# A hybrid decoder layer on one core: the first norm on two token tiles at a time, with another first chunk of projection weights

## The reference, cut to what matters

```python
def reference(x, mix_norm, w_in, ...):              # x: 1 x 512 x 1024, float32
    h = rms_norm(x, mix_norm)                       # the first norm: one root per token
    z = h @ w_in                                    # columns aq ak av iq ik iw pin gu gv sq sk sv gl
    o_a = sparse_indexed_attention(aq, ak, av, iq, ik, iw, ...)   # indexer scores, top 128 keys, attention
    o_b = multiscale_pool(pin, ...)
    o_c = chunked_spatial_gating(gelu(gu), gelu(gv), ...)
    o_d = stick_breaking_attention(sq, sk, sv)
    x = x + (sum of sigmoid(gl_n) * (o_n @ w_branch[n])) @ w_out
    return x + swiglu_ffn(rms_norm(x, ffn_norm), w_ffn_gate, w_ffn_up, w_ffn_down)

# the indexer of branch A, for each block of 128 queries:
head_scores = relu(einsum('bthd,bsd->bths', q_idx, k_idx))        # 8 heads
idx_score = einsum('bth,bths->bts', w_idx, head_scores)
```

## Time and profile before

| | |
|---|---|
| median of 3 runs | 811.78 us |
| the profiled execution | 811.23 us, of which the span from first to last instruction is 809.3 us |
| TensorE (PE) busy | 789.0 us, 97% of the span |
| VectorE (DVE) busy | 502.2 us, 62% |
| ScalarE (ACT) busy | 375.8 us, 46% |
| GpSimd (POOL) busy | 59.3 us, 7% |
| matmuls | 4713 |
| DMA | 80.36 MB, mean 99 GB/s |

### The profile page before, as it was taken

The page is one execution under the profiler, slowest core; times in us unless marked ns, Lnnn a source line. Parts: engine busy times, 40 slices in busy tenths (PEclk is TensorE's granted clock), DMA queues, the critical chain, the costliest instruction groups (busy, mean ns, idle before and its releaser), DMA issues.

```text
span 809.3 us, 11519 instructions
## 1 busy us (share of the span) xinstructions
PE 789.0 (97%) x4713; PEld 692.5 (86%) x4713; DVE 502.2 (62%) x743; ACT 375.8 (46%) x525; POOL 59.3 (7%) x71
## 2 busy tenths in 40 slices
PE   3999999999999999999989999999999999999998
PEld 3899887877778878878878889999988899999886
DVE  5535987656577566361284699888633478887331
ACT  5435544577845533522233465555521245554210
POOL 6000040000000050050060000000000000000000
PEclk9999999999999999999999999999999999999999
DMA  8452213121122313513314213333232233333321
GB/s 256 123 164 67 92 53 104 53 96 62 53 59 97 104 53 104 208 54 104 104 53 150 85 53 122 111 110 111 101 125 91 74 97 104 106 104 104 120 89 52
DMA packets 63763, 80.36 MB, mean 99 GB/s; under 512 B 1684, under 2 KB 51936, under 8 KB 63712
## 3 DMA queue, kind: packets, MB, share of 16 engines
q1 hardware_dynamic: 63376, 79.18, 30.6%
q0 software_dynamic: 336, 0.46, 0.2%
HBM read 75.96 MB, written 2.10 MB: 96 GB/s over the span
## 4 chain that ended last, share of the span: by engine, by line
PE 78%; issue 13%; POOL 3%; DVE 3%; ACT 1%; DMA 1%; SPq 0%; POOLq 0%; DVEq 0%
PE bank L1378 16%; PE bank L1380 16%; PE bank L1379 16%; PE bank L1745 8%; PE bank L1747 8%; PE bank L1746 8%; POOL merged L483 3%; PE bank L1544 1%; PE bank L1553 1%; DMA x_sb<-in_x_dram 1%; DVE w_lo L863 1%; PE bank L1484 1%; PE bank L1458 0%; PE bank L1528 0%; ACT h_hi L527 0%
## 5 line engine op out<-in xcount | busy, mean ns | idle before, releaser
L863 DVE TENSOR_TENSOR w_lo<-raw,w_hi 128x2048 fp32r<-128x2048 f32 (+1 forms) x45 | 100.2, 2228 | 121.1 <-ACT w_hi L503 120.8
L1378 PE MATMUL bank<-h_hi,w_hi 128*128 128x512 f32 (+1 forms) x392 | 150.7, 385 | 0.7 <-DVE h_lo L1186 0.5
L1380 PE MATMUL bank<-h_hi,w_lo 128*128 128x512 f32 (+1 forms) x392 | 149.3, 381 | 0.0
L1379 PE MATMUL bank<-h_lo,w_hi 128*128 128x512 f32 (+1 forms) x392 | 149.1, 380 | 0.0
L503 ACT ACTIVATE w_hi<-raw 128x2048 fp32r<-128x2048 f32 (+1 forms) x49 | 91.1, 1861 | 89.0 <-PE bank L1380 88.1
L1745 PE MATMUL bank<-t_hi,w_hi 128*128 128x256 f32 x320 | 89.7, 280 | 0.0
L1746 PE MATMUL bank<-t_lo,w_hi 128*128 128x256 f32 x320 | 89.3, 279 | 0.0
L1747 PE MATMUL bank<-t_hi,w_lo 128*128 128x256 f32 x320 | 89.3, 279 | 0.0
L1378 PEld LDWEIGHTS bank<-h_hi,w_hi 128*128 128x128 f32 x392 | 73.7, 188 | 15.4 <-issue 1.3
L1380 PEld LDWEIGHTS bank<-h_hi,w_lo 128*128 128x128 f32 x392 | 73.7, 188 | 14.3
L1379 PEld LDWEIGHTS bank<-h_lo,w_hi 128*128 128x128 f32 x392 | 73.7, 188 | 13.6
(11 more groups left out here) (232 smaller groups left out, 1473.5 us busy)
## 6 DMA issues: line engine op xcount, KB each, us to landing
raw<-in_w_in_dram SPq DMA_DIRECT2D x26, 1024.0 KB, 5.2
raw<-in_w_ffn_gate_dram SPq DMA_DIRECT2D x11, 1024.0 KB, 5.3
raw<-in_w_ffn_up_dram SPq DMA_DIRECT2D x11, 1024.0 KB, 5.3
raw<-in_w_ffn_down_dram SPq DMA_DIRECT2D x10, 1024.0 KB, 5.0
raw<-in_w_branch_dram SPq DMA_DIRECT2D x4, 1024.0 KB, 4.8
raw<-in_w_out_dram SPq DMA_DIRECT2D x4, 1024.0 KB, 5.1
x_sb<-in_x_dram SPq DMA_DIRECT2D x4, 512.0 KB, 5.0
x_sb<-in_x_dram SPq DMA_DIRECT2D x1, 2048.0 KB, 10.5
```

Source lines behind the costliest of these rows:

```text
L863: vec.tensor_tensor(w_lo[:, at], raw[:, c % 2, 0:n], w_hi[:, at].bitcast(F32), ALU.subtract)\
L1378: mm(dst, l_hi, r_hi, start=start, stop=False)
L1379: mm(dst, l_hi, r_lo, start=False, stop=False)
L1380: return mm(dst, l_lo, r_hi, start=False, stop=stop)
```

## The change

`aq` becomes chunk 0, of a new kind "first"; `ik` and `iq` become chunks 1 and 2, and from `ak` (3) on the numbers stay. The first norm is made on token tiles 0 and 1, then on tiles 2 and 3, and each half is followed by its half of the matmuls of `aq`. `aq` is loaded in two halves, right behind tiles 0 and 1 of x; the seven loads of `vrow` go to GpSimd's queue. IDX_SLOT becomes 3, so that the indexer's blocks stand in slots 3, 4, 5, the early splits are those of chunks 5 to 8, and in chunk 6 (rows, two parts) both pairs of heads stand between the parts. The turns of slot 1 go to slot 2. `gv` and `gu` get another place in SBUF. Waits that count squares are moved by one, since there is one more square on ScalarE.

```diff
+    chunks.append(("first", in_cols(w_in, col["aq"]), KT, CW, "aq"))
     chunks.append(("rows", in_cols(w_in, col["ik"], P), KT, P, "ik"))
     chunks.append(("rows", in_cols(w_in, col["iq"]), KT, CW, "iq"))
-    for n in ("aq", "ak", "av", "gv"):
+    for n in ("ak", "av", "gv"):
...
-        gv = place("gv", [P, TT, MIX], at=X0)
-        gu = place("gu", [P, MT, SEQ], at=X0 + 4 * KB)
...
+        gv = place("gv", [P, TT, MIX], at=L0 + 44 * KB)
+        gu = place("gu", [P, MT, SEQ], at=L0 + 48 * KB)
         act_junk = place("act_junk", [P, 2, D], at=L0)
-        dve_junk = place("dve_junk", [P, 2, D], at=L0 + 20 * KB)
+        dve_junk = place("dve_junk", [P, 1, D], at=L0 + 20 * KB)
...
-        IDX_SLOT = 2
+        IDX_SLOT = 3
...
-            for t in range(TT):
+            def load_x(t):
                 sp.dma_start(x_sb[:, t, :], x[0, t * P:(t + 1) * P, :]).then_inc(x_ready[t], 16)
+            def load_first(half, ready):
+                src = chunks[0][1][:, half * KT // 2:(half + 1) * KT // 2, :]
+                dst = raw[:, 0, half * CHUNK // 2:(half + 1) * CHUNK // 2].rearrange("p (k c) -> p k c", c=CW)
+                sp.dma_start(dst, src).then_inc(ready, 16)
 
             def load(c):
                 _, src, nk, cols, _ = chunks[c]
@@ -367,18 +374,17 @@
                 dst = raw[:, c % 2, 0:nk * cols].rearrange("p (k c) -> p k c", c=cols)
                 sp.dma_start(dst, src).then_inc(raw_ready[c % 2], 16)
 
-            load(0)
-            sp.dma_start(vrow[0:KT, :], mix_norm[0].rearrange("(k p) -> k p", p=P)).then_inc(S["vec_in"], 16)
-            sp.dma_start(vrow[PSC:PSC + MT, :], pool_scale[0].rearrange("(k p) -> k p", p=P)).then_inc(S["vec_in"], 16)
-            sp.dma_start(vrow[GMN:GMN + MT, :], gmlp_norm[0].rearrange("(k p) -> k p", p=P)).then_inc(S["vec_in"], 16)
-            for r, g in ((QN, attn_q_norm), (KN, attn_k_norm)):
-                for j in range(2):
-                    sp.dma_start(vrow[r:r + 1, j * HEAD_DIM:(j + 1) * HEAD_DIM], g).then_inc(S["vec_in"], 16)
+            load_x(0)
+            load_x(1)
+            load_first(0, S["w_first"])
+            load_first(1, raw_ready[0])
+            load_x(2)
+            load_x(3)
             for c in range(1, MIXER_CHUNKS):
                 load(c)
                 if c == 4:
 
-                    wait_chunk_taken(sp, 1)
+                    wait_chunk_taken(sp, 2)
...
+            pool.dma_start(vrow[0:KT, :], mix_norm[0].rearrange("(k p) -> k p", p=P)).then_inc(S["vec_in"], 16)
+            pool.dma_start(vrow[PSC:PSC + MT, :], pool_scale[0].rearrange("(k p) -> k p", p=P)).then_inc(S["vec_in"], 16)
+            pool.dma_start(vrow[GMN:GMN + MT, :], gmlp_norm[0].rearrange("(k p) -> k p", p=P)).then_inc(S["vec_in"], 16)
+            for r, g in ((QN, attn_q_norm), (KN, attn_k_norm)):
+                for j in range(2):
+                    pool.dma_start(vrow[r:r + 1, j * HEAD_DIM:(j + 1) * HEAD_DIM], g).then_inc(S["vec_in"], 16)
...
-            for t in (0, 2):
+            def squares_of(t):
                 act.wait_ge(x_ready[t], 16)
-                nact.activation(act_junk[:, t // 2, :], x_sb[:, t, :], ACT.Square, accum_out=stat[:, t:t + 1])\
+                nact.activation(act_junk[:, t % 2, :], x_sb[:, t, :], ACT.Square, accum_out=stat[:, t:t + 1])\
                     .then_inc(S["squares_summed"], 1)
-            take_root(slice(0, TT))
-            split(0)
-            act.wait_ge(S["rstd_ready"], 1)
-            nact.activation(x_sb[:, TT - 1, :], x_sb[:, TT - 1, :], ACT.Copy, scale=rstd[:, TT - 1:TT])\
-                .then_inc(S["h_last_scaled"], 1)
+            def scaled(t):
+                act.wait_ge(S["rstd_ready"], t // 2 + 1)
+                nact.activation(x_sb[:, t, :], x_sb[:, t, :], ACT.Copy, scale=rstd[:, t:t + 1])\
+                    .then_inc(S["h_last_scaled"], 1)
+            def first_high(half, arrived):
+                at = slice(half * CHUNK // 2, (half + 1) * CHUNK // 2)
+                act.wait_ge(arrived, 16)
+                nact.activation(w_hi[:, at], raw[:, 0, at], ACT.Copy).then_inc(hi_ready if half else S["first_hi"], 1)
+            def h_high(half, ks):
+                cols = slice(half * SEQ // 2, (half + 1) * SEQ // 2)
+                for k in ks:
+                    n = half * KT + k
+                    act.wait_ge(S["h_turned"], n + 1)
+                    nact.activation(h_hi[:, k, cols], bank[4 + n % 4][:, 0:SEQ // 2], ACT.Copy,
+                                    scale=vcol[:, MIXN + k:MIXN + k + 1]).then_inc(S["h_hi_ready"], 1)
+            squares_of(0)
+            take_root(slice(0, 2))
+            first_high(0, S["w_first"])
+            scaled(1)
             act.wait_ge(S["vec_turned"], 1)
-            link(nact.activation(vcol[:, :], bank[1][:, 0:VECS], ACT.Copy))
-            for k in range(KT):
-                act.wait_ge(S["h_turned"], k + 1)
-                nact.activation(h_hi[:, k, :], bank[2 + k % 6][:, :], ACT.Copy, scale=vcol[:, MIXN + k:MIXN + k + 1])\
-                    .then_inc(S["h_hi_ready"], 1)
+            link(nact.activation(vcol[:, :], bank[3][:, 0:VECS], ACT.Copy))
+            h_high(0, range(0, KT // 2))
+            first_high(1, raw_ready[0])
+            h_high(0, range(KT // 2, KT))
+            squares_of(2)
+            squares_of(3)
+            take_root(slice(2, 4))
+            scaled(3)
+            h_high(1, range(KT))
...
+                if kind == "first":
+                    for t in range(TT):
+                        act.wait_ge(filled, t // 2 + 1)
+                        ins = nact.activation(qk[:, 0, t, :], bank[t][:, 0:MIX], ACT.Copy)
+                        if t < 2:
+                            ins.then_inc(taken[t], 1)
+                    return
...
+            def first_low(half):
+                at = slice(half * CHUNK // 2, (half + 1) * CHUNK // 2)
+                dve.wait_ge(hi_ready if half else S["first_hi"], 1)
+                vec.tensor_tensor(w_lo[:, at], raw[:, 0, at], w_hi[:, at].bitcast(F32), ALU.subtract)\
+                    .then_inc(lo_ready if half else S["first_lo"], 1)
+            def h_low(half, ks):
+                cols = slice(half * SEQ // 2, (half + 1) * SEQ // 2)
+                for k in ks:
+                    n = half * KT + k
+                    dve.wait_ge(S["h_hi_ready"], n + 1)
+                    vec.scalar_tensor_tensor(out=h_lo[:, k, cols], in0=bank[4 + n % 4][:, 0:SEQ // 2],
+                                             scalar=vcol[:, MIXN + k:MIXN + k + 1], in1=h_hi[:, k, cols].bitcast(F32),
+                                             op0=ALU.mult, op1=ALU.subtract).then_inc(S["h_lo_ready"], 1)
+            def normed(half, squares):
+                ts = slice(2 * half, 2 * half + 2)
+                dve.wait_ge(S["squares_summed"], squares)
+                vec.tensor_scalar(stat[:, ts], stat[:, ts], 1.0 / D, EPS, ALU.mult, ALU.add).then_inc(S["var_ready"], 1)
+                inverse_root(ts)
+                vec.tensor_scalar(x_sb[:, 2 * half, :], x_sb[:, 2 * half, :], rstd[:, 2 * half:2 * half + 1], None, ALU.mult)\
                     .then_inc(S["h_scaled"], 1)
-            split(0)
-            for k in range(KT):
-                dve.wait_ge(S["h_hi_ready"], k + 1)
-                vec.scalar_tensor_tensor(out=h_lo[:, k, :], in0=bank[2 + k % 6][:, :],
-                                         scalar=vcol[:, MIXN + k:MIXN + k + 1], in1=h_hi[:, k, :].bitcast(F32),
-                                         op0=ALU.mult, op1=ALU.subtract).then_inc(S["h_lo_ready"], 1)
+            dve.wait_ge(x_ready[1], 16)
+            link(vec.tensor_tensor_reduce(out=dve_junk[:, 0, :], in0=x_sb[:, 1, :], in1=x_sb[:, 1, :],
+                                          scale=1.0, scalar=0.0, op0=ALU.mult, op1=ALU.add, accum_out=stat[:, 1:2]))
+            normed(0, 1)
+            first_low(0)
+            h_low(0, range(0, KT // 2))
+            first_low(1)
+            h_low(0, range(KT // 2, KT))
+            normed(1, 3)
+            h_low(1, range(KT))
...
-            def rows_chunk(c, cols, bank_of):
+            def rows_chunk(c, cols, bank_of, between=None):
                 for j in range(cols // P):
+                    if j and between is not None:
+                        between(1)
+                        between(2)
...
+            nc.tensor.transpose(bank[3][:, 0:VECS], vrow[:, :], ident[0:VECS, 0:VECS]).then_inc(S["vec_turned"], 1)
+            def turn_h(half, k):
+                n = half * KT + k
+                if n >= 4:
+                    pe.wait_ge(S["h_lo_ready"], n - 3)
+                for i, scaled in ((0, S["h_scaled"]), (1, S["h_last_scaled"])):
+                    if k == 0:
+                        pe.wait_ge(scaled, half + 1)
+                    last = nc.tensor.transpose(bank[4 + n % 4][:, i * P:(i + 1) * P],
+                                               x_sb[:, 2 * half + i, k * P:(k + 1) * P], ident[:, :])
```

(83 more changed lines are left out.)

2 lines of the change are left out of this document (1 added, 1 removed).

## The result

The changed kernel takes **816.38 us** (median of 4 runs, 815.04 to 817.18) against 811.70 us of the kernel before: ratio 1.0055, 95% interval 1.0037 to 1.0072. It is slower by 4.7 us, where the forecast was 816.1 and slower. In its profiled execution (815.04 us) the span is 813.3 us, 4.0 more than before.

What follows compares the result with a forecast made beforehand. The prediction took TensorE's full list behind an empty start as the bound. Terms of -0.2, +1.4 and +3.1 gave +4.3, or 816.1 us on the median; own range 814.3 to 817.6, with rivals 812.8 to 818.3.

Steps and rivals of the forecast that it cites:

- The start: Up to the turns behind `iq`: first product at 12.9 instead of 18.3, yet only 0.2 us gained.
- The hole: Between the first norm's halves, TensorE has only 8 transposes from 20.2 to 24.0: 3.8 us, 2.9 net.
- The indexer's first heads: Block 1: chunk 5's late load delays its split and the relus on ScalarE; TensorE waits 1.4 us.
- Block 3 against the norms: Before chunk 7: norm sums delay block 3, relus and table loads delay the gelu of `gu`; TensorE waits 3.1 us.
- The sum: Whole kernel: -0.2 + 1.4 + 3.1 = +4.3 us, giving 816.1 us on the median.
- Rival (a): Between the first norm's halves the clock falls and the second half starts slowly: 1.7 us, 817.8 us; chance 0.15.
- the gelu wait: Before chunk 7, TensorE waits for a bank until the gelu of `gu`'s first part is done: 3.1 us.
- (b): Before chunk 7: VectorE reaches block 3 three us earlier, hiding the wait on the gelu; +1.2, 813.0 us; chance 0.13.
- (c): At the start, the gap between the halves closes: -3.1 us, 810.1 us if the gelu's wait is hidden too; chance 0.06.
- (d): At the start, `vrow` lands at 12.5 or later, moving the first half by 1.7: 817.8 us; chance 0.06.
- third wait: Behind chunk 7: none forecast; one on VectorE between 100 and 130 us would show the prediction wrong.

Runs made afterwards that it cites:

- f_squares: Changed kernel with the squares of tiles 2 and 3 brought forward at the start, tile 3 on VectorE; 814.77 us, ratio 1.0042 to the kernel before.
- after_again: The changed kernel timed once more, nothing altered; 816.34 us, ratio 1.0049 to the kernel before.
- a_late: Changed kernel with chunk 5 split one chunk later on ScalarE and VectorE; 814.31 us, ratio 1.0033 to the kernel before.
- a_root: Changed kernel with slot 5's root and a gelu table load moved between relus 3 and 4 of block 3 on ScalarE; 814.99 us, ratio 1.0032.
- b_slot3: Kernel before with only the indexer one slot later and what that needs, old start kept; 815.02 us, ratio 1.0041.
- a_both: Changed kernel with the edits of a_late and a_root together; 812.15 us, ratio 0.9996 to the kernel before.
- g2_sums: a_both with squares and sums of `aq` and `ak` between the splits of chunks 5 and 6 on VectorE; 811.91 us, ratio 0.9998 to the kernel before.
- g_sums: a_both with squares and sums of `aq` and `ak` behind the indexer's block 1, ahead of chunk 5's split; 814.71 us, ratio 1.0036.

## Why the prediction was right, point by point

**The start, -0.2 forecast, -0.4 measured.** Most steps hold. `vrow` landed at 10.2 rather than 10.8 to 11: a load of GpSimd's queue took 4.5 to 5.4 from issue to landing. The first product came at 12.76 (12.9 forecast), the second half's tiles at 22.0 (22.2), its first products at 24.0 (24.1), the turns behind `iq` at 46.84 (47.1). Not six but eleven products ran at the slow pace, which ended at 15.7, and half one was through at 20.5 and not 20.2; the earlier landing made up for it. The hole was as forecast: f_squares takes part of it out and gains that part. That the result comes within 0.2 us is partly luck: in after_again's profile of the same kernel `vrow` landed at 11.7, the slow pace lasted until 18.0, and the turns came at 48.69, so the start lost 1.4 us against the profile of before, where the first one gained 0.4. One pair of profiles does not settle a term of this size.

**The indexer's first heads, +1.4 forecast.** The load of chunk 5 was issued at 56.29 and the split began 5.4 us later; TensorE's wait in the list is 1.1, and what it costs is some 0.4 more: around it the starts stand 1.42 apart (62.53 to 63.95) where like products stand 0.12 apart, and the pair of heads behind it takes 0.50 and not 0.24. Its removal (a_late) gave 2 us of the median, with other shares of slow clock in the two sets of runs; in the traces, from the turns behind `iq` to chunk 7, it is 1.6.

**Block 3 against the norms, +3.1 forecast, 2.6 in the list, some 2.8 in the distance of starts.** The mechanism is shown by a_root and, in the old start, by b_slot3. The term was 0.3 us too large: I took VectorE's end of block 2 at +11.0 behind chunk 4 from a row with a wait of 0.53 us for a relu in it, and in the changed kernel that block ran without it (78.96, seven in 4.95) and ended at +10.6 (chunk 4 ends at 73.33).

**The sum, +4.3.** The traces give +4.0, and one fall of the clock costs 1.4 to 1.7 in them. That the median says +4.7 is not the same thing: two of its four runs have a fall of the clock, which the sum left out. At full clock the change costs 3.0; the two sets of its runs, with a fall in half of each, say 4.7 and 4.4. By those prices a fall in half of the runs is worth about the 0.7 us that the median has over the traces. That 816.1 came so near to 816.38 is therefore in part luck: the terms were 0.3 us too large together, and the falls of the clock, which no term holds, put some 0.7 on the other side.

**Rival (a), the clock falls in the hole.** It did not there: on the far side transposes are 0.11 apart, and the granted clock is 1.00. The mechanism exists, at other places: the clock fell in half of the runs, and in the one of these that was profiled it fell behind the gelu wait. I had priced it at the hole and did not ask the same of the 3.1 us wait, which is longer unbroken idle time than the hole has in one piece (1.4), nor of the 2.0 us wait that both kernels have. That is the step in which the prediction was incomplete; the range held it.

**Rivals (b), (c), (d)** fall: the gelu wait is there, the hole did not close, `vrow` was not late. What the forecast said of the time behind chunk 7 holds for the changed kernel, where no third wait showed. It does not hold once the gelu wait is out (a_root, a_both): then VectorE's list is the bound and collides with GpSimd.

What stays open: why the clock falls in ten of twelve runs of g2_sums and in none of eleven of a_both. Both have the same waits between the halves and the same 2.0 us on `two`, and that one stands in the kernel before too, with a fall in 2 of 51 runs. No run of g2_sums with a fall was profiled. Falls were seen behind waits of 2.0 us (416 to 419, in a_late, a_root and g_sums) and 2.6 us, none behind the hole of the halves; the length of the wait alone does not decide it, and what does was not tried.

## What to carry to other kernels

When a piece of work is moved by one slot in a hand-ordered kernel, follow each engine's list and not only the one that wins: here one index moved by one put a load in front of a split in front of relus, and 5 us of squares and sums and two table loads in front of an evacuation, and that cost more than the new start gave. An earlier start is worth only what is left of it further on; look for the hole behind it. And where TensorE waits as long as it did here (2.0 to 2.6 us), the forecast needs a second term with a chance of its own, the slow stretch that followed in some executions and cost 1.4 to 1.7 us.

## What the runs showed of the hardware that I had not expected

- The clock of TensorE falls to 1.2 GHz in the midst of a full list, behind a wait of 2.0 to 2.6 us, and comes back while the list goes on. It does so in some executions of the same program and not in others, and costs 1.4 to 1.7 us each time by the traces. The stretches of g_sums (columns as for after_again) around the end of the 2.0 us wait, with TensorE busy throughout the second:

```profile
415.50:418.00 2.50, 0.54 (x2) 0.48 (x3) 2.50 (x4) 0.63 (x1) 0.74 (x2) 1.00 0.03 9
418.80:421.80 3.00, 3.00 (x8) 2.30 (x7) 3.00 (x4) 1.26 (x2) 3.00 (x3) 0.50 0.81 313
```

- VectorE and GpSimd, each on a float32 operation with two operands in SBUF, seem not to have worked side by side in a_both (109.8 to 115.7): two sums of 1.94 us and a split of 2.29 are 6.2 us alone and took 5.9 together. The ends fit whole operations in turn: first sum until 111.77, split until 113.92 (2.15 later), second sum until 115.72 (1.80 later); each one's recorded time then includes its wait for the other. That is a reading of one stretch (and of a_root, with 3.97 and 3.87), not a test. VectorE's top-k operations did not slow GpSimd: in the changed kernel they run beside the first sum and the start of the second, which take 1.94 each.
- The moment at which TensorE reaches 2.4 GHz at the start moves from execution to execution. The products of half one go from 0.21 us apart to 0.12 at 13.7 us in a_root, at 15.7 in the changed kernel's first profile and at 18.0 in after_again, with the first transposes at 10.0, 10.2 and 11.7. Second half and later chunks of after_again were up to 1.9 us later than in the first profile of the same kernel, of which 1.5 was the later landing of `vrow`.
